# Two-layer decoder with experts on one core: the rows of the next expert are gathered by matmuls with a selection matrix and no longer by a trip through DRAM

## The reference

```python
def moe_swiglu(x, router, w13, w2):
    logits = (x @ router).astype(jnp.float32)
    top_vals, top_idx = lax.top_k(logits, TOP_K)          # TOP_K = 2, N_EXPERTS = 8
    top_w = jax.nn.softmax(top_vals, axis=-1)
    gates = jnp.einsum('bsk,bske->bse', top_w, jax.nn.one_hot(top_idx, N_EXPERTS, dtype=jnp.float32))
    out = jnp.zeros_like(x)
    for e in range(N_EXPERTS):
        out = out + gates[..., e:e + 1].astype(x.dtype) * swiglu(x, w13[e], w2[e])
    return out
```

## Time and profile before

| | |
|---|---|
| time, median of 3 executions | 1701.49 us (1701.23 to 1701.55) |
| time of the profiled execution | 1701.23 us |
| its span, first to last instruction | 1699.4 us |
| PE busy | 1666.1 us, 98% of the span |
| DVE busy | 1366.5 us, 80% |
| ACT busy | 1041.9 us, 61% |
| POOL busy | 29.3 us, 2% |
| shares of the chain that ended last | PE 89%, DVE 8%, DMA 1% |
| one pass of the expert loop on PE, from a block of its chain (1117.03) to the same block one pass later (1237.60) | 120.57 us |
| transfers of `xa_wkv` halves, median from issue to landing | 5.1 us |
| moved | 478.61 MB, mean 282 GB/s |
| mean granted TensorE clock | 0.995 of 2.4 GHz |

### The profile page before, as it was taken

How to read it: one execution, slowest core, us unless ns; L and a number is a source line. 1 busy time by engine, 2 the same in 40 slices (tenths; PEclk the granted TensorE clock), 3 DMA queues, 4 the chain that set the end, 5 groups by cost and what they waited for, 6 DMA issues and landing times.

```text
span 1699.4 us, 21961 instructions
## 1 busy us (share of the span) xinstructions
PE 1666.1 (98%) x8126; PEld 1379.5 (81%) x8126; DVE 1366.5 (80%) x1264; ACT 1041.9 (61%) x917; POOL 29.3 (2%) x37
## 2 busy tenths in 40 slices
PE   8999999999999999999999999999999999999996
PEld 7887888888887888878888888888888888888885
DVE  4788756545666886699899898898898998998997
ACT  4564444434345544377777777777777777777774
POOL 0001000000000100010000000000000000000000
PEclk9999999999999999999999999999999999999998
DMA  8523446546454545599999999999999999999992
GB/s 298 167 97 104 169 131 215 175 148 223 173 198 175 197 149 199 176 346 398 389 383 376 356 383 371 354 386 366 361 382 368 358 378 367 370 379 353 380 371 94
DMA packets 211001, 478.61 MB, mean 282 GB/s; under 512 B 14496, under 2 KB 17344, under 8 KB 210752
## 3 DMA queue, kind: packets, MB, share of 16 engines
q1 hardware_dynamic: 209952, 475.69, 77.1%
q0 software_dynamic: 576, 2.10, 0.3%
q10 hardware_dynamic: 416, 0.04, 0.0%
HBM read 474.65 MB, written 9.44 MB: 285 GB/s over the span
## 4 chain that ended last, share of the span: by engine, by line
PE 89%; DVE 8%; DMA 1%; issue 1%; ACT 1%; DVEq 0%; SPq 0%; ACTq 0%
PE ps L2357 51%; PE ps L1792 22%; PE ps L2212 4%; DVE w_lo L1102 2%; PE ps L1831 2%; PE ps L1835 2%; PE ps L2339 1%; PE ps L1752 1%; PE ps L2132 1%; PE ps L2113 1%; DVE qk L1348 1%; DVE ring_r L1090 1%; PE ps L1987 1%; DMA ring<-in_xa_wkv_dram 1%; DVE late L1242 1%
## 5 line engine op out<-in xcount | busy, mean ns | idle before, releaser
L1102 DVE TENSOR_TENSOR w_lo<-ring,w_hi 128x2048 fp32r<-128x2048 f32 x336 | 766.2, 2289 | 88.9 <-ACT w_hi L756 86.7
L756 ACT CAST w_hi<-ring 128x2048 fp32r<-128x2048 f32 x336 | 641.2, 1911 | 243.3 <-PE ps L2357 241.2
L2357 PE MATMUL ps<-w_hi,xe_hi 128*128 128x512 f32 x896 | 243.7, 394 | 0.2 <-DVE xe_lo L1599 0.2
L2357 PE MATMUL ps<-w_lo,xe_hi 128*128 128x512 f32 x896 | 240.4, 390 | 2.5 <-DVE w_lo L1102 2.5
L2357 PE MATMUL ps<-w_hi,xe_lo 128*128 128x512 f32 x896 | 239.9, 389 | 0.0
L2357 PEld LDWEIGHTS ps<-w_lo,xe_hi 128*128 128x128 f32 x896 | 167.7, 188 | 39.4 <-DVE w_lo L1102 4.8
L2357 PEld LDWEIGHTS ps<-w_hi,xe_lo 128*128 128x128 f32 x896 | 168.2, 188 | 35.8
L1792 PE MATMUL ps<-ring_r,xT_r 128*128 128x512 f32 (+1 forms) x736 | 193.9, 392 | 2.4 <-ACT ring_r L723 1.7
L2357 PEld LDWEIGHTS ps<-w_hi,xe_hi 128*128 128x128 f32 x896 | 165.2, 188 | 32.3 <-DVE xe_lo L1599 0.2
L1792 PEld LDWEIGHTS ps<-ring_r,xT_r 128*128 128x128 f32 x736 | 135.0, 188 | 34.2 <-ACT ring_r L723 2.2
L2357 PE MATMUL ps<-w_hi,he_hi 128*128 128x512 f32 x448 | 141.7, 397 | 0.0
(11 more groups left out here) (319 smaller groups left out, 1923.6 us busy)
## 6 DMA issues: line engine op xcount, KB each, us to landing
ring<-in_moe_w_dram SPq DMA_DIRECT2D x336, 1024.0 KB, 6.6
ring<-in_ffd_w_dram SPq DMA_DIRECT2D x31, 1024.0 KB, 5.0
ring<-in_w_in_dram SPq DMA_DIRECT2D x23, 1024.0 KB, 5.3
ring<-in_xa_wkv_dram SPq DMA_DIRECT2D x16, 1024.0 KB, 5.1
ring<-in_w_out_dram SPq DMA_DIRECT2D x8, 1024.0 KB, 5.0
ring<-in_xa_wq_dram SPq DMA_DIRECT2D x8, 1024.0 KB, 5.0
ring<-in_xa_wo_dram SPq DMA_DIRECT2D x8, 1024.0 KB, 5.0
sent_rows<-in_zeros_dram SPq DMA_DIRECT2D x12, 512.0 KB, 7.1
```

Of the source, the lines that this page charges most:

```text
L756: act.copy(w_hi[:, q % SPLIT_SLOTS, :], ring[:, RAW_ORDER[q % RAW_SLOTS], :]).then_inc(hi_ready, 1)
L1102: dve.tensor_tensor(w_lo[:, q % SPLIT_SLOTS, :], ring[:, RAW_ORDER[q % RAW_SLOTS], :], w_hi[:, q % SPLIT_SLOTS, :].bitcast(F32), ALU.subtr ...
L2357: ins = pe.matmul(ps[:, bank, :], xs[:, k, :], w[:, c, cols], start=(first and m == 0), stop=(last and m == 2))
```

## The change

The trip through DRAM goes, and every item's rows are gathered as item 0's were. `sel` for item i + 1 is made by DVE at q = 20 of item i (two TENSOR_SCALARs of 128 x 128, ahead of the two for `back`), and PE runs `gather` at the places of `turn_rows`: after q = 33 and after q = 37, each with eight float32 matmul calls (four blocks of features, two token tiles) in place of four transposes. Nothing else of the order of work is changed.

```diff
@@ bass_decoder: tensors and semaphores
-        row = sb("row", [P, T, NE])
-        row_of = sb("row_of", [P, 2, T])
-        row_i = sb("row_i", [P, 2, T], I32)
-        row_step = sb("row_step", [P, 2, NE])
-            xg = sbe("xg", [P, D])
-        sent = nc.dram_tensor("sent_rows", (NE + EXTRA + 1, P, D), F32).ap()
@@ SP
-            def clear_rows(part):
-
-                each = (NE + EXTRA + 1) // KV_P
-                for n in range(each * part, each * (part + 1)):
-                    sp.dma_start(sent[n], a["zeros"]).then_inc(rows_cleared, 16)
-
-            def load_rows(i):
-
-                sp.dma_start(xg[:, :], sent[i]).then_inc(rows_in, 16)
...
-                    if l == DEPTH - 1 and IN_P <= n < IN_P + KV_P:
-                        clear_rows(n - IN_P)
...
-                    if first and q == 24:
-                        sp.wait_ge(rows_out, 16 * 2 * T)
-                        load_rows(1)
-                    if not first and q == 12:
-                        sp.wait_ge(misc_ready[0], 5 * i + 1)
-                        load_rows(i + 1)
@@ POOL
-                    if l == DEPTH - 1 and n == 2 * T:
-                        send_rows()
@@ DVE
+            def select(i):
+
+                for t in range(T):
+                    ins = dve.tensor_scalar(sel[:, t, :], place, slot[:, t, bass.ds(i, 1)], None, ALU.is_equal)
+                ins.then_inc(sel_ready, 1)
...
-                    if first and q == 9:
-                        row_places()
                     if q == 20:
+                        select(i + 1)
                         for t in range(T):
                             ins = dve.tensor_scalar(back[:, t, :], place, slot[:, t, bass.ds(i, 1)], None, ALU.is_equal)
                         ins.then_inc(back_ready, 1)
@@ PE
-            def turn_rows(i, j, g):
-
-                pe.wait_ge(rows_in, 16 * i + 16)
+            def gather(i, j, g, count):
+
+                pe.wait_ge(sel_ready, count)
                 b = misc_bank(j, i)
                 for c in range(4):
-                    k = 4 * g + c
-                    ins = pe.transpose(ps[:, 6 + b, c * P:(c + 1) * P], xg[:, k * P:(k + 1) * P], ident)
+                    for t in range(T):
+                        k = 4 * g + c
+                        ins = pe.matmul(ps[:, 6 + b, c * P:(c + 1) * P], x[:, t, k * P:(k + 1) * P], sel[:, t, :],
+                                        start=(t == 0), stop=(t == T - 1))
                 ins.then_inc(misc_ready[b], 1)
...
                     if q == 33:
-                        turn_rows(i, 7, 0)
+                        gather(i, 7, 0, i + 2)
                     if q == 37:
-                        turn_rows(i, 8, 1)
+                        gather(i, 8, 1, i + 2)
```

More of the change, by code:

```diff
@@ L152, in shape_constants @@
     rows = np.broadcast_to(rows[None, :], (P, rows.size)).astype(np.float32)
-    zeros = np.zeros((P, D), np.float32)
-    return {"zeros": zeros, "mask_a": mask_a, "mask_b": mask_b, "level": level, "square": square,
+    return {"mask_a": mask_a, "mask_b": mask_b, "level": level, "square": square,
             "rows": np.ascontiguousarray(rows)}
@@ L344, in bass_decoder @@
         oa_taken, dilated_taken = sem("oa_taken"), sem("dilated_taken")
-        rows_cleared, rows_known, rows_out, rows_in = (
-            sem(name) for name in ("rows_cleared", "rows_known", "rows_out", "rows_in"))
         dec_diff, dec_exp = sem("dec_diff"), sem("dec_exp")
@@ L642, in power @@
                 pool.tensor_tensor(rstd[:, c], var[:, c], mhalf[:, c], ALU.pow).then_inc(rstd_ready, 1)
[L644 to L653, removed]
             for l in range(DEPTH):
@@ L1654, in extra_items @@
                     dve.sem_inc(table_ready, 1)
[L1656 to L1668, removed]
             def take_y(i, halves=range(2)):
```

## The result

| | before | changed |
|---|---|---|
| first measurement, median | 1701.36 us (1698.52 to 1701.55, 4 executions) | 1716.74 us (1715.92 to 1717.49, 4 executions) |
| second measurement, median | 1700.16 us (1698.29 to 1702.75, 21) | 1716.46 us (1716.37 to 1718.10, 4) |
| profiled execution, span | 1699.4 us | 1714.7 us |
| mean granted clock of the profiled execution | 0.995 | 0.998 |

The change makes the kernel slower by about 1.0%: the ratio is 1.0095 with a 95% interval of 1.0080 to 1.0109 in the first measurement, and 1.0098 (1.0083 to 1.0114) in the second. In microseconds that is 14 to 19; the forecast was 17.5 and the time forecast 1718.7, in a range of 1716.2 to 1722.2.

The account below looks back on a forecast made before the run. The prediction took PE to bound the kernel's expert stage. Gathers +21.6, clears -2.4 and item 0 -1.7 made +17.5 us on the profiled 1701.23: 1718.7 us, range 1716.2 to 1722.2.

Parts of the forecast that it names:

- PE as the bound of the expert stage: Expert stage, items 1 to 7: PE's added work lengthens the run by just that; relieving other queues brings nothing.
- The rival in which transfers set the pace: Expert stage: DMA limits each item, so longer gathers cost nothing and items get shorter; 1687 us, chance 0.02.
- The gather's price: PE, two gathers in each of eight items: 1.80 us each for 0.45 of transposes, +21.6 us.
- The price by the Trainium skill's pages: PE's gathers: four passes per float32 call at 81 ns, 2.6 us a gather, +34 us; not used in the sum.
- The clears: Layer 1 mixer: without clears ahead of an `xa_wkv` half, a 2.36 us wait and 1.41 us of slow clock go; -2.4 net.
- that dip: Layer 0's 3.4 us at clock 0.50, 35 us further on; expected in layer 1 too, charged at 1.4 us.
- The rival without a second dip: Layer 1: the clock does not dip a second time, all else as forecast; 1717.3 us, chance 0.23.
- the term of -2.4: Layer 1 mixer: -3.8 us for the wait and clock dip that go, +1.4 for a later dip.
- `row_places`: DVE, item 0: its 2.14 us go and PE's two waits for `w_lo` shrink to about nothing; -2.0 us.
- the bound of 2.14: Item 0: DVE's whole time on `row_places`, the upper end of that gain; the two waits, 1.88, were the lower.
- `select`: DVE, q = 20 of each item: 0.56 us of work, costing nothing in items 1 to 7 and 0.3 in item 0.

Follow-up runs that it names:

- the gathers alone: Kernel before with the gathers and `select` put in and the whole trip through DRAM left in, its reload unread: 1722.00 us, ratio 1.0134.
- the POOL edit: Kernel before with the arithmetic of `row_places` done by POOL in place of DVE; with the clears where they were: 1699.90 us, ratio 0.9998.
- the kernel with the clears in layer 0: Kernel before with the twelve clears issued in layer 0 in place of layer 1, after the same four panels: 1698.89 us, ratio 0.9998.
- `select` later: Changed kernel with `select` at q = 26 in place of q = 20: 1717.32 us in one execution.
- `row_places` later: Kernel before with `row_places` at q = 25 of item 0 for q = 9, and SP's wait and reload at q = 34 for 24: 1699.66 us, ratio 1.0004.
- the clears moved alone: Kernel before with the twelve clears, four each, behind the second to fourth `xa_wkv` panels of layer 1: 1697.12 us, then 1696.48.
- both edits: Kernel before with clears behind the second to fourth `xa_wkv` panels of layer 1 and the arithmetic of `row_places` on POOL: 1697.36 us, then 1695.94.

## Why the prediction was right

**PE as the bound of the expert stage: right.** The 22 us that PE got to do came out as 22 us of time, and the reload, the scatter and their waits gave nothing back, as the earlier trace rows had said. The rival in which transfers set the pace is excluded by the gathers alone, with all transfers left in: passes of 123.24 us.

**The gather's price: right in its mechanism, a little small in its size.** The forecast was 16 x 1.35 = 21.6. The block itself was 1.79 us for 1.80 forecast. Per pass it came to 2.79 for 2.70; the gathers alone gave 2.67. The remaining 0.1 us of the changed kernel lie between its large matmuls (48 of them take 10.93 us, where the gathers alone have 10.90 to 10.92), like the 0.06 of the POOL edit; their cause is open. Eight times 2.8 make 22.4.

**The price by the Trainium skill's pages: too dear.** Two measurements, 1.79 us for eight calls and 0.90 for four, give 0.22 us a call, or 56 ns for each of the four passes that the prediction counts in it. A float32 call of 128 columns costs PE about as much here as one of its reduced-form matmuls of 512 (0.2275). The spacing of 81 ns that the Trainium skill gives for streams of 128 columns (TensorE: Matmul & The Clock Gate, "Back-to-back issue gap"), taken for each of those passes, had made 2.6 us of a gather; these runs don't agree.

**The clears: the wait right, the clock wrong.** Theory and size of the wait hold (2.36 us forecast to go; 6.53 against 4.20 us with the clears moved to layer 0). What failed is the step "if layer 1 becomes like layer 0, it gets that dip in exchange". Nine of the thirteen profiled executions of the kernels of this study have no wait there in layer 1, and none of the nine has a stretch at 0.50 from 563 to 571. The one near 125 us was there in five of the thirteen (the kernel before, `select` later, and the three with the POOL edit), though the program up to there is the same in all but the kernel with the clears in layer 0. It costs 1.5 us: from the first transposes of `turn_heads` in layer 0 to the six transposes at 129 the five take 43.81 to 43.86 us, the seven others with that program 42.29 to 42.34. The one near 531 was there only in the trace of the kernel before, though three other kernels had the same wait (2.1 to 2.3 us). One of them, with `row_places` later, at 529.8 to 533.2:

```profile
529.80:533.20 3.40, 3.08 (x28) 2.71 (x28) 1.94 (x6) 1.87 (x2) 0.72 (x1) 1.00 0.68 252
```

That kernel takes 6.63 us from transposes to scores, for 7.86 in the kernel before, whose wait is 0.11 us longer; the stretch near 531 cost the 1.1 that are left, not the 1.41 that the prediction had for it.

So the trace that the forecast was worked from held two such stretches, 2.6 us, and the one of the changed kernel none. From the forecast's 17.5 to the 15.3 between the two spans it goes like this: -3.6 in layer 1 for -2.4, -1.5 in layer 0 for nothing, -2.0 in item 0 for -1.7, and 22.4 for the gathers instead of 21.6. Without such stretches in either, the sum is 22.4 - 2.0 - 2.4 = +18.0 us: 22.4 for the gathers, -2.0 for what else changed in item 0, and 6.63 - 4.23 = 2.4 for the wait. The fastest executions of the two kernels (1698.2 and 1715.9) lie 17.7 apart. The rival without a second dip (1717.3) came nearer to the measured time than the forecast (1718.7). Luck had a part in it: the term of -2.4 was put together from a stretch that goes and one that comes in exchange, and that it equals what the wait alone is worth is chance; and the measured 1716.74 lies only half a microsecond inside the range.

Whether there is such a stretch changes from execution to execution of one kernel, as far as the times show it: in the second measurement of the clears moved alone, six executions lie from 1695.9 to 1696.5 and five from 1697.5 to 1697.9, with nothing between. So the chance of 0.23 for "no second dip" had been put on the wrong question. What stays open is whether the wait makes a stretch more frequent. Before the second measurement of the changed kernel +18 us had been expected if both kernels have as many, and +16.6 if the one near 531 goes with the wait; the medians came out 16.3 apart, and 15.4 the first time. The clears moved alone gained 2.6 and 3.6 us for a wait of 2.4. Both speak for it. Against it stand the traces: one of four with the wait in layer 1 has the stretch.

**`row_places`: right.** -2.0 forecast, -2.2 by the starts of PE's matmuls, and -2.1 when POOL took the work over. The middle was taken where the bound of 2.14 was nearer, as DVE was late throughout.

**`select`: right.** Nothing in the passes; in item 0 0.3 us had been forecast, and moving it to q = 26 took 0.2 away. With one execution of that version this rests on the trace alone.

## What to carry to other kernels

A matmul used as a gather is no cheap move on an engine that is the bound: price it by records (0.11 us each here, with 8 columns as with 128) and compare with the transposes that it replaces, which take half the calls and half the records of each call. The parts of the trip through DRAM that nobody waited for cost nothing here; where such a trip costs something, look at what it was queued ahead of, and move that before giving up the trip. And before a forecast is made against one trace, look in it for stretches at half clock, and compare the medians of many executions: the stretches may be that execution's alone.

## What the runs showed that was not expected

- TensorE's clock fell to 0.50 for 3.4 us in five traces at a place where seven others, of the same program up to there, kept 1.00, all behind an idle time of about 1.3 us; it cost 1.5 us. Much of the spread of the kernel before (1698.2 to 1702.8) would be explained by none, one or two such stretches. Why a stretch falls in one execution and not in another is open. All three traces with the POOL edit had it, and no kernel was traced once with and once without it, so a part of the program in it is not excluded. The mean clock of an execution doesn't count them: every trace also ends with 8 to 11 us at 0.50, behind PE's last matmul, where it costs nothing, and that difference moves the mean as much as one stretch does.
- An edit on POOL and DVE in item 0 shifted PE's pace by about 0.8 us in a stretch 200 us earlier. Differences under about 1 us between programs say nothing here unless the trace shows a wait.
- POOL's smallest operations come in two sizes, 0.2 and 2.1 us, on the same few elements. The same ones are long in all three traces with the POOL edit; the cause is open. From its timeline in the kernel with both edits:

```profile
741.54 2.11 POOL L658 TENSOR_SCALAR row_step<-row_step 128x8 f32<-128x8 f32 x1
743.73 0.20 POOL L659 TENSOR_SCALAR row_step<-rows 128x8 f32<-128x8 f32 x1
744.00 0.27 POOL L660 TENSOR_SCALAR row<-slot 128x16 f32<-128x16 f32 x1
744.36 2.11 POOL L661 TENSOR_TENSOR row<-row,row_step 128x16 f32<-128x16 f32 x1
```
